# Projections of a fused two-block kernel: the forget/gate panel, its row sum and three kinds of DMA issues moved to earlier places

## What is computed

```
h = rms_norm(x, g_attn)
z = h @ w_in                      # all projections at once
(fq, fk, fv, f_logit, nq, kc, vc, ksl, vsl, kwn, vwn, n_gate, g_a, g_b) = split(z)
o_fox = fox_attention(fq, fk, fv, f_logit, b_forget)   # scores + running sum of log sigmoid(f_logit + b)
o_nsa = nsa_attention(nq, kc, vc, ..., n_gate, rel_bias_table, cmp_*)   # three branches, each times sigmoid(n_gate)
x = x + (sigmoid(g_a) * (o_fox @ w_br_fox) + sigmoid(g_b) * (o_nsa @ w_br_nsa)) @ w_out
```

## Time and profile before

| | before |
|---|---|
| median of 3 runs | 1728.22 us |
| lowest, highest | 1727.46, 1730.08 us |
| the profiled execution, its own time | 1731.71 us |
| its span, first to last instruction | 1729.9 us |
| mean granted TensorE clock | 0.985 of full speed |
| TensorE busy | 1641.7 us (95%) |
| VectorE, ScalarE, GpSimd busy | 1118.3, 716.5, 165.0 us |

### The profile page before, as it was taken

One profiled execution on the slowest core, in us unless ns is written; L12 is line 12 of the kernel. 1 busy time (PEld: TensorE's weight loads), 2 busy tenths in 40 slices (PEclk: granted clock), 3 DMA queues, 4 the chain that ended last, 5 costly groups with the idle time before them and its releaser, 6 DMA issues.

```text
span 1729.9 us, 22027 instructions
## 1 busy us (share of the span) xinstructions
PE 1641.7 (95%) x7956; PEld 1344.5 (78%) x7956; DVE 1118.3 (65%) x1763; ACT 716.5 (41%) x1232; POOL 165.0 (10%) x187
## 2 busy tenths in 40 slices
PE   7998889988999999999989999999899899999997
PEld 5877666766788888788867787888678888888886
DVE  6754787886576675763578479998665644444456
ACT  5353775555443132312443244444534432232232
POOL 0012300000030000000002980000000000000000
PEclk9999999999999999999999999999999999999998
DMA  4346831111535555542213221221332233232332
GB/s 158 121 121 172 182 75 44 43 57 49 195 135 169 206 188 188 192 137 74 85 49 126 93 64 53 62 62 50 92 122 76 84 97 97 91 95 93 98 98 97
DMA packets 49969, 185.43 MB, mean 107 GB/s; under 512 B 6928, under 2 KB 9232, under 8 KB 47456
## 3 DMA queue, kind: packets, MB, share of 16 engines
q1 hardware_dynamic: 39600, 136.76, 24.4%
q0 software_dynamic: 10288, 47.60, 9.4%
HBM read 172.23 MB, written 6.85 MB: 104 GB/s over the span
## 4 chain that ended last, share of the span: by engine, by line
PE 75%; DVE 14%; ACT 5%; issue 3%; DMA 2%; SPq 0%; ACTq 0%; DVEq 0%
PE ps L1996 17%; PE ps L1998 16%; PE ps L1997 16%; PE ps L2058 2%; PE ps L2059 2%; PE ps L2060 2%; DVE w_lo L1174 2%; DMA raw<-in_panels 1%; PE ps L2412 1%; PE ps L2411 1%; PE ps L2413 1%; PE ps L2245 1%; ACT w_hi L668 1%; PE ps L2206 1%; PE ps L2247 1%
## 5 line engine op out<-in xcount | busy, mean ns | idle before, releaser
L1996 PE MATMUL ps<-h_hi,w_hi 128*128 128x512 f32 x832 | 329.2, 396 | 9.5 <-DVE h_lo L1664 3.7
L1998 PE MATMUL ps<-h_hi,w_lo 128*128 128x512 f32 x832 | 323.9, 389 | 0.0
L1997 PE MATMUL ps<-h_lo,w_hi 128*128 128x512 f32 x832 | 323.9, 389 | 0.0
L1174 DVE TENSOR_TENSOR w_lo<-raw,w_hi 128x1024 fp32r<-128x1024 f32 x181 | 227.6, 1260 | 117.1 <-ACT w_hi L668 91.0
L601 ACT ACTIVATE w_hi<-raw 128x1024 fp32r<-128x1024 f32 x125 | 131.3, 1051 | 170.5 <-DMA raw<-in_panels 170.4
L1996 PEld LDWEIGHTS ps<-h_hi,w_hi 128*128 128x128 f32 x832 | 156.2, 188 | 49.9 <-DVE h_lo L1664 5.8
L1997 PEld LDWEIGHTS ps<-h_lo,w_hi 128*128 128x128 f32 x832 | 156.2, 188 | 33.4 <-issue 1.9
L1998 PEld LDWEIGHTS ps<-h_hi,w_lo 128*128 128x128 f32 x832 | 156.2, 188 | 32.7
L1996 PE MATMUL ps<-f_hi,w_hi 128*128 128x512 f32 x408 | 166.8, 409 | 0.0
L1998 PE MATMUL ps<-f_hi,w_lo 128*128 128x512 f32 x408 | 161.3, 395 | 0.0
L1997 PE MATMUL ps<-f_lo,w_hi 128*128 128x512 f32 x408 | 160.9, 394 | 0.0
(11 more groups left out here) (422 smaller groups left out, 3356.2 us busy)
## 6 DMA issues: line engine op xcount, KB each, us to landing
raw<-in_panels SPq DMA_DIRECT2D x252, 512.0 KB, 3.6
wm<-in_w_mod POOLq DMA_DIRECT2D x16, 1536.0 KB, 7.8
scratch_r<-r POOLq DMA_DIRECT2D x8, 320.0 KB, 9.7
bias<-scratch_c POOLq DMA_DIRECT2D x8, 256.0 KB, 9.1
kd<-k_hi POOLq DMA_DIRECT2D x16, 128.0 KB, 4.1
kd<-k_lo POOLq DMA_DIRECT2D x16, 128.0 KB, 5.1
bias<-scratch_r POOLq DMA_DIRECT2D x8, 256.0 KB, 3.0
X<-in_x POOLq DMA_DIRECT2D x1, 2048.0 KB, 9.7
```

The lines of the kernel that those rows point to most:

```text
L1174: dve.tensor_tensor(w_lo[:, n % RING], raw[:, n % RING], w_hi[:, n % RING].bitcast(F32), ALU.subtract)\
L1996: pe.matmul(out, w_hi[:, u, b, :], hi[:, k, :N], start=start, stop=False)
L1997: pe.matmul(out, w_hi[:, u, b, :], lo[:, k, :N], start=False, stop=False)
L1998: ins = pe.matmul(out, w_lo[:, u, b, :], hi[:, k, :N], start=False, stop=stop)
```

## The change

The diff, whole but for unchanged lines. Panel "low" becomes panel 11 (from 17), c0 to c3 stand earlier, the ScalarE chain up to the logarithm moves to step "c1" (behind the high part of panel 14) and the sigmoid to step "v0" (behind the high part of panel 15); VectorE's running sum moves to step "v0", ahead of the value of "v0"; TensorE turns both after panel "v0" and folds after panel "s1"; the GpSimd queue is reordered.

```diff
-PROJ = ["kc", "vc", "q0", "q1", "q2", "q3", "k0", "k1", "k2", "k3", "c0", "v0", "v1", "c1", "v2", "v3", "c2", "low",
-        "s0", "c3", "s1", "v4", "c4", "v5", "n0", "c5", "n1", "c6", "n2", "c7", "n3", "none"]
+PROJ = ["kc", "vc", "q0", "q1", "q2", "q3", "k0", "k1", "k2", "c0", "k3", "low", "c1", "v0", "v1", "c2", "v2", "v3",
+        "c3", "s0", "s1", "c4", "v4", "v5", "c5", "n0", "n1", "c6", "n2", "c7", "n3", "none"]
-TURN_AFTER = {"v1": 0, "v2": 1, "v3": 2, "low": 3, "v5": 4, "n0": 5}
+TURN_AFTER = {"v1": 0, "v2": 1, "v3": 2, "s0": 3, "v5": 4, "n0": 5}
 GpSimd
-        gp.wait_ge(sem("c_summed"), 1)
-        gp.dma_start(scratch_c, cum[:]).then_inc(sem("rows_stored"), 16)
+        gp.wait_ge(sem("rel_rows"), 2)
+        for n in range(8):
+            gp.wait_ge(used, done(AT["q2"] + n))
+            gp.dma_start(scratch_r[:, n * REL_ROWS:(n + 1) * REL_ROWS, :],
+                         r8[:].unsqueeze(1).to_broadcast([8, REL_ROWS, 640])).then_inc(sem("rel_stored"), 16)
...
-        for n in range(2):
-            gp.wait_ge(sem("kn_split"), n + 1)
-            for g in range(2):
-                both_halves(kn_hi[n][g], g, sem("kn_doubled"))
-                both_halves(kn_lo[n][g], g, sem("kn_doubled"))
-        gp.wait_ge(sem("v_turned"), 5)
-        gp.dma_start(w2k[:], a["w2k"]).then_inc(sem("w2_loaded"), 16)
-        gp.dma_start(w2v[:], a["w2v"]).then_inc(sem("w2_loaded"), 16)
...
-        gp.wait_ge(sem("rows_stored"), 16)
-        for n in range(16):
-            if n == 8:
-                gp.wait_ge(sem("rel_stored"), 16 * 8)
+        def bias_rows(n):
...
+        fox_keys(0)
+        gp.wait_ge(sem("c_summed"), 1)
+        gp.dma_start(scratch_c, cum[:]).then_inc(sem("rows_stored"), 16)
+        gp.dma_start(w2k[:], a["w2k"]).then_inc(sem("w2_loaded"), 16)
+        gp.dma_start(w2v[:], a["w2v"]).then_inc(sem("w2_loaded"), 16)
+        gp.wait_ge(sem("rows_stored"), 16)
+        bias_rows(0)
+        bias_rows(1)
+        for n in range(2):
+            gp.wait_ge(sem("kn_split"), n + 1)
+            for g in range(2):
+                both_halves(kn_hi[n][g], g, sem("kn_doubled"))
+                both_halves(kn_lo[n][g], g, sem("kn_doubled"))
+        fox_keys(1)
+        for n in range(2, 16):
+            if n == 8:
+                gp.wait_ge(sem("rel_stored"), 16 * 8)
+            bias_rows(n)
             if n < 8:
                 fox_keys(n)
-                gp.wait_ge(sem("rel_rows"), 2)
-                gp.dma_start(scratch_r[:, n * REL_ROWS:(n + 1) * REL_ROWS, :],
-                             r8[:].unsqueeze(1).to_broadcast([8, REL_ROWS, 640])).then_inc(sem("rel_stored"), 16)
 ScalarE, in the step
-            if name == "low":
+            if name == "c1":
                 act.wait_ge(sem("forget_z"), 1)
                 chain(act.activation(lf_a[:], zf[:], ACT.Abs))
                 chain(act.activation(lf_a[:], lf_a[:], ACT.Exp, scale=-1.0))
                 act.activation(lf_a[:], lf_a[:], ACT.Ln, bias=cst[0:8, C_ONE:C_ONE + 1]).then_inc(sem("forget_ln"), 1)
+            if name == "v0":
                 act.wait_ge(sem("proj_val"), ORDER["low"] + 1)
                 act.activation(sig_n[:], gate_v[:], ACT.Sigmoid).then_inc(sem("gate_n"), 1)
...
-            if name == "c5":
+            if name == "n0":
                 act.wait_ge(sem("cmp_k_out"), 1)
 VectorE, in the step, right behind panel_lo(n + AHEAD)
+            if name == "v0":
+                dve.wait_ge(sem("forget_z"), 1)
+                dve.wait_ge(sem("forget_ln"), 1)
+                chain(dve.scalar_tensor_tensor(zf[:], zf[:], 0.0, lf_a[:], ALU.min, ALU.subtract))
+                chain(dve.tensor_scalar(zf[:], zf[:], -S8, None, ALU.mult))
+                chain(dve.memset(lf_a[:], 1.0))
+                dve.tensor_tensor_scan(cum[:], lf_a[:], zf[:], 0.0, ALU.mult, ALU.add).then_inc(sem("c_summed"), 1)
+            if name == "v1":
+                dve.wait_ge(sem("c_turned"), 1)
...
+                dve.wait_ge(sem("gate_turned"), 1)
+                dve.tensor_copy(gate_t[:], ps[:, 5, 0:96].rearrange("p (t h) -> p t h", h=24)).then_inc(sem("gate_t_ready"), 1)
 (the same two blocks go from steps "s0" and "v4", where they stood behind the value of the panel)
 TensorE: turn_v
-            if j in (2, 3):
+            if j >= 2:
                 pe.wait_ge(sem("v_lo_done"), j - 1)
-            elif j == 4:
-                pe.wait_ge(sem("gate_t_ready"), 1)
-            elif j == 5:
-                pe.wait_ge(sem("c_q_ready"), 1)
+            else:
+                pe.wait_ge(sem("c_q_ready" if j else "gate_t_ready"), 1)
 turn_c and turn_gate lose their waits on v_lo_done; in the loop over the panels
-            if name == "s1":
+            if name == "v0":
                 turn_c()
                 turn_gate()
-            if name == "v4":
+            if name == "s1":
                 fold(0)
-            if name == "n0":
+            if name == "v5":
                 pe.wait_ge(sem("w2_loaded"), 32)
                 pe.wait_ge(sem("cmp_hidden"), 1)
```

More of the change, by code:

```diff
@@ L1268, in _ @@
                 panel_lo(n + AHEAD)
+            if name == "v0":
[7 more added lines that the diff above has]
+                dve.wait_ge(sem("c_turned"), 1)
+                dve.tensor_scalar(c_q8[:], ps[:, 4, 0:32].rearrange("p (t h) -> p t h", h=8), -1.0, None, ALU.mult)\
+                   .then_inc(sem("c_q_ready"), 1)
+                dve.wait_ge(sem("gate_turned"), 1)
+                dve.tensor_copy(gate_t[:], ps[:, 5, 0:96].rearrange("p (t h) -> p t h", h=24)).then_inc(sem("gate_t_ready"), 1)
             if name == "low":
@@ L2091, in turn_c @@
         def turn_c():
-            pe.wait_ge(sem("v_lo_done"), 3)
             pe.wait_ge(sem("c_summed"), 1)
@@ L2099, in turn_gate @@
         def turn_gate():
-            pe.wait_ge(sem("v_lo_done"), 4)
             pe.wait_ge(sem("gate_n"), 1)
```

## The result

| | before | changed |
|---|---|---|
| median | 1727.84 us (4 runs) | 1746.34 us (4 runs) |
| lowest, highest | 1727.26, 1730.08 us | 1743.76, 1750.72 us |
| ratio, 95% interval | 1 | 1.011 [1.0091, 1.0128] |
| span of the profiled execution | 1729.9 us | 1742.0 us |

The change makes the kernel 18.5 us slower. The forecast was 1.7 us faster, and its range ended at 1731.

The account below looks back on a forecast made before the run. With TensorE busy 95% of the span, only its idle gaps and lower-clock time could be won: 12.7 us removed, 11.0 added, -1.7 us against the median of 1728.22, so 1726.5 us, range 1722.0 to 1731.0.

Parts of the forecast that it names:

- Moved at no cost: Table blocks sent as panels 4 to 11 end: panels may take 9.6 us to land; up to 1.7 us each, counted as none.
- cover: Panel loads beside the early blocks: slack before need; a stall before "v0" ends shortens the 5.6 us wait unless reaching the chain.
- Both gaps of before: TensorE's waits for panels' low parts, 3.99 and 4.09 us, with 2.9 and 1.7 us of low clock: 12.7 us removed.
- The second gap: TensorE's 4.09 us gap from a 9.70 us panel load; removed because panels 24 to 30 then load alone, at 3.5 us.
- Wait for the running sum: TensorE after "v0", in front of the transpose of the sum: a new wait of 5.6 us.
- its clock term: Lower TensorE clock after the running sum's wait: 2.9 us added, 1.7 us kept for the range.
- Wait for the compression sums: TensorE after "s1", in front of the first fold: a new wait of 2.5 us, covered by panel "v4" before.
- The clock doesn't fall behind the 2.5 us gap: TensorE after the compression sums' wait: clock loss taken as 0, with 2.9 us as the upper bound.
- the 2.8 us: ScalarE's two table switches ahead of the logarithm: by the skill's drain the sum comes 2.8 us later; not counted, no drain seen.
- The fox heads: Heads after the projections: no gain counted from moving the blocks; a rival had 2 to 5 us from quieter DMA, chance 0.13.
- the second rival: ScalarE's high part of panel 15 waits for its load: +1.5 to +3.1 us against before, 1729.7 to 1731.3, chance 0.18.

Follow-up runs that it names:

- f_spaced: The changed kernel with the 8 table blocks, still from 8 partitions, sent as every second panel ends: 1732.49 us, ratio 1.0023 to the kernel before.
- c2_dram: The changed kernel with the blocks sent at the same moments but read from DRAM, where one 20 KB DMA puts the rows first: 1728.89 us, ratio 1.0001.
- a_blocks_late: The changed kernel with the blocks back between the heads' keys, two behind the second head's: 1734.18 us, ratio 1.0031 to the kernel before.
- h_cum_fixed_dram: The changed kernel with early blocks from DRAM and the running sum turned behind c2, the fold still behind s1: 1721.45 us, ratio 0.9958.
- g_fixed_dram: The changed kernel with early blocks from DRAM, running sum turned behind c2, compression sums folded behind v4: 1716.78 us, ratio 0.9939 to the kernel before.
- d_both_fixed: `a_blocks_late` with the running sum and gates turned behind c2 and the compression sums folded behind v4: 1722.56 us, ratio 0.9971 to the kernel before.
- a2_one_per_head: The changed kernel with one block behind the keys of each of the 8 heads: 1731.61 us, ratio 1.0022 to the kernel before.
- c_by_head: The changed kernel, same bytes and moments, each block DMA writing 128 rows of one head from one partition: 1794.45 us, ratio 1.0389.

## Why the prediction was wrong

**The step that failed is "Moved at no cost".** It took the landing times of before (9.7 us, the median of the blocks, to 11.3 us, the worst panel) as the worst that a block could do to a panel. That left at most 1.7 us a panel beyond the 9.6 us that it may take, and the step put even this at nothing. Those landings were measured with the blocks 7.6 us or more apart. The change sends six of them within 20.3 us, mostly 5.4 us apart, while one holds its source for some 6.4 us (`f_spaced`). They piled up: panels landed in 10.6 to 23.7 us from 45 to 90 us, the blocks in 15.0 us in the median. The trace of before could have told it, asked for a stretch in which a block moves alone, 143.8 to 145.3 us:

```profile
DMA packets 16, 0.08 MB, mean 55 GB/s; under 512 B 0, under 2 KB 0, under 8 KB 16
...
q0 software_dynamic: 16, 0.08, 51.1%
```

At 55 GB/s a block needs some 6.0 us (an estimate from 0.08 MB), and that doesn't fit into 5.4.

The price is the difference between `c2_dram` and the changed kernel, which send the same bytes at the same moments: ratios 1.0001 and 1.011, 19 us. In the traces the first fold after "s1" comes at 123.51 and at 141.09, 17.6 us apart: the four gaps are 15.2 us of it, the wait for the sum is 2.0 us shorter (5.34 to 3.33), and the rest is 17.6 - 15.2 + 2.0 = 4.4 us. The lower clock accounts for most of it: behind 75.21 nine matmuls take 3.67 us where 2.04 would do, behind 93.49 thirteen take 5.60 us where 2.95 would do, 1.6 + 2.7 us.

The step also counted on cover: a stall ahead of the end of "v0" shortens the wait for the sum unless it reaches the chain itself. Both happened. The late panels pushed "v0" back, but VectorE also scaled "low" only at 93.37, 5.5 us after TensorE had ended it, because the low part of a late panel stood in front. So the wait got only 2.0 us shorter, and the gaps were 15 us. The sign that the prediction named for the slow side, gaps for panel loads between 47 and 90 us, is what came.

**The other terms, one by one.** The waits held; the clock terms did so only in part.
- Both gaps of before are gone in every run with the new order. The second gap is not seen anywhere: panels after "v4" land in 4 us in the median.
- Wait for the running sum: forecast 5.6 us, measured 5.34 us (`c2_dram`) and 5.35 us (`a_blocks_late`). With its clock term the wait was priced at 5.3 + 2.9 = 8.2 us in the expectation of `h_cum_fixed_dram`; from `c2_dram` to that run it is 7.4 us by the ratios.
- Wait for the compression sums: forecast 2.5 us, measured 2.49 us in six traces.
- Sum without the blocks' cost: forecast -1.7 us; `c2_dram` has a ratio of 1.0001 [0.9992, 1.0010], -1.4 to +1.7 us, so the forecast lies just outside. In its trace the heads do start 3.8 us earlier than before (first row maximum at 172.32 against 176.12), and 1.6 us of this go again right there, where the clock falls behind the gap of 1.87 us: from its end to the end of the next gap (for `sb`) 13.39 us against 11.81. Both waits away: forecast 11.0 us, measured 12.1 us from `c2_dram` to `g_fixed_dram`, 11.6 us from `a_blocks_late` to `d_both_fixed`.
- "The clock doesn't fall behind the 2.5 us gap": it did in three traces of six (`a_blocks_late`, `a2_one_per_head`, `h_cum_fixed_dram`) and didn't in the others (the changed kernel, `c2_dram`, `c_by_head`). Its ground, that a gap of 1.86 us left the clock up, was a single case: behind this very gap of 1.86 or 1.87 us at the start of the heads the granted clock fell to 1.2 GHz in six of the twelve traces. The term should have been a mean between 0 and the bound, not 0.
- No drain was seen around the table loads: in `c2_dram` the Abs row ends at 77.50 and the load begins at 77.52, the load ends at 78.80 and Exp begins at 78.81. So the 2.8 us that the prediction drew from the Trainium skill ("ScalarE: Activation LUTs", What ACT_TABLE_LOAD costs) stay out.
- The fox heads: no gain from the quieter engines was found; apart from the late keys of `a_blocks_late` and `d_both_fixed`, the waits at their start are the same in all runs (0.91 us for `row_max`, 1.86 or 1.87 us for `gate_z`). What differs is the clock behind them, and not with the traffic: it fell in `c2_dram`, without any block beside the heads, and stayed up there in the kernel before.

The right direction stood among the rivals, but with the wrong size and place: the second rival was one panel's load against one block and four keys, up to 3.1 us. Its mechanism was real (`a2_one_per_head`: 8.96 us, 2.56 us late); the same mechanism several times over, earlier and with no pause, was what decided.

Left open: which part of the path makes reading few partitions slow, their port, the partition's memory or the many requests to one address. The runs tell the number of source partitions (1, 8, or none) apart, not these; no run reads few partitions without repeating them. In `c2_dram` too a row is read 128 times, so repetition alone, out of DRAM, isn't slow.

## What to carry to other kernels

A landing time is no service time: before a transfer is moved to a tighter spacing, compare the spacing with the time that one takes, its bytes over the rate at which it moves when it is alone. The row of the queue over such a stretch tells it: few bytes beside a large share of the DMA engines is the sign, and a broadcast out of few SBUF partitions is the kind to suspect. Such a broadcast is cheaper by way of DRAM: write the few rows once and copy them from there. And when an extra is moved to an earlier step of a written-out order, count what stands in front of it on each queue, since TensorE waits at the new place for the whole chain.

## What the hardware showed unexpectedly

- Copying 320 KB to DRAM took 35.0 us in the median out of one SBUF partition, 15.0 us out of eight (9.1 us with 6.4 us or more between them) and 4.7 us out of DRAM. The engine time for a megabyte was 536, 249 and 48 us. One partition gave 27 GB/s; eight gave 51 GB/s with 48.3% of the engines' time and 53 GB/s with 83.8%.
- The panel loads on the other queue paid for it in full: 42.2, 20.2 and 3.7 us in the median in the same window. The Trainium skill ("DMA: Bandwidth & Descriptors", Queues, rings and completion order) has each engine take turns between its queues packet by packet; by that rule a panel's packets each wait for one slow packet of the other queue, which agrees with the direction of these rows; no run measures the turns themselves.
- Behind a gap of TensorE of 2.49 us, the same instructions found the clock at 1.2 GHz in three traces and at 2.4 GHz in three. Behind one of 1.86 or 1.87 us at the start of the heads it was six and six: after 1.2 GHz the stretch to the end of the next gap took 13.39 us (`c2_dram`), after 2.4 GHz 11.81 us (before).
